# First layer norm of a one-core decoder step: output weights centred before the projection, variance per token, logits from the unscaled sum

## The reference, cut to what matters

```python
merged = g_a * y_a + g_b * y_b + g_c * y_c
m = merged @ w_o
h = layer_norm(ALPHA * x + m, ln1_g, ln1_b)        # mean, variance, rsqrt(var + 1e-5), gain, bias
logits = h @ router_w + router_b                   # (520, 16), softmax, best group of 4, top 2
for e in range(16):
    out += gates[:, e:e+1] * ((silu(h @ w_gate[e]) * (h @ w_up[e])) @ w_down[e])
y = layer_norm(ALPHA * h + out, ln2_g, ln2_b)
```

## Time and profile before

| | us |
|---|---|
| median of 3 runs (lowest, highest) | 1100.54 (1098.97, 1101.18) |
| the profiled execution | 1099.52 |
| its span | 1097.7 |
| TensorE busy | 1001.4 (91%) |
| VectorE busy | 797.5 |
| ScalarE busy | 476.3 |
| GpSimd busy | 349.9 |

### The profile page before, as it was taken

The page is one execution under the profiler, slowest core; times in us unless marked ns, Lnnn a source line. Parts: engine busy times, 40 slices in busy tenths (PEclk is TensorE's granted clock), DMA queues, the critical chain, the costliest instruction groups (busy, mean ns, idle before and its releaser), DMA issues.

```text
span 1097.7 us, 19553 instructions
## 1 busy us (share of the span) xinstructions
PE 1001.4 (91%) x7141; PEld 901.5 (82%) x7141; DVE 797.5 (73%) x960; ACT 476.3 (43%) x661; POOL 349.9 (32%) x268
## 2 busy tenths in 40 slices
PE   6999999999998899999999988974999999999950
PEld 6999999999998789999999988943677777776630
DVE  2398889988898796734335443346789898989969
ACT  3222222222222153335432221263788888787820
POOL 2444444444544242444545443302110000000050
PEclk9999999999999899999999998986999999999985
DMA  7433233323332121422332337655799999999552
GB/s 200 117 97 95 80 93 96 94 82 91 96 96 67 57 87 48 131 88 85 94 98 77 95 89 260 242 213 184 246 358 392 378 381 379 389 391 367 183 195 109
DMA packets 169539, 189.86 MB, mean 173 GB/s; under 512 B 5875, under 2 KB 121587, under 8 KB 169484
## 3 DMA queue, kind: packets, MB, share of 16 engines
q1 hardware_dynamic: 162987, 177.46, 47.9%
q0 software_dynamic: 3008, 10.55, 3.0%
q10 hardware_dynamic: 3505, 1.36, 0.5%
HBM read 178.57 MB, written 11.76 MB: 173 GB/s over the span
## 4 chain that ended last, share of the span: by engine, by line
PE 78%; DVE 10%; issue 4%; DMA 4%; ACT 1%; SPq 1%; POOL 1%; DVEq 0%; POOLq 0%; ACTq 0%
PE pr L891 53%; PE pr L1029 13%; PE work L1029 7%; DVE acc_a L1221 2%; DMA y_rows<-y_out 1%; DMA sb_tok<-in_state_conv_b_dram 1%; PE work L1013 1%; POOL y_a L600 1%; PE work L976 1%; PE work L967 1%; DMA hs<-h_rows,ids 1%; DVE acc_b L1221 1%; PE work L953 1%; DVE stats L1550 1%; DVE y_a L1548 1%
## 5 line engine op out<-in xcount | busy, mean ns | idle before, releaser
L532 POOL TENSOR_TENSOR w_lo<-raw,w_hi 128x512 fp32r<-128x512 f32 x224 | 303.7, 1377 | 394.8 <-ACT w_hi L628 394.8
L891 PE MATMUL pr<-x_hi,w_hi 128*128 128x260 f32 x1280 | 260.1, 284 | 3.1 <-POOL w_lo L532 3.1
L891 PE MATMUL pr<-x_hi,w_lo 128*128 128x260 f32 x1280 | 259.4, 284 | 0.0
L891 PE MATMUL pr<-x_lo,w_hi 128*128 128x260 f32 x1280 | 259.2, 284 | 0.0
L632 ACT ACTIVATE ev<-pr 128x520 f32<-128x520 f32 x104 | 63.0, 605 | 436.3 <-PE pr L891 436.2
L891 PEld LDWEIGHTS pr<-x_hi,w_hi 128*128 128x128 f32 x1280 | 199.4, 190 | 3.5 <-DVE x_lo L1136 3.3
L891 PEld LDWEIGHTS pr<-x_hi,w_lo 128*128 128x128 f32 x1280 | 199.0, 190 | 0.0
L891 PEld LDWEIGHTS pr<-x_lo,w_hi 128*128 128x128 f32 x1280 | 198.4, 190 | 0.0
L1188 DVE SCALAR_TENSOR_TENSOR work<-b_pad,par,work 128x512 f32<-128x512 f32 x224 | 148.2, 746 | 0.0
L628 ACT ACTIVATE w_hi<-raw 128x512 fp32r<-128x512 f32 x224 | 128.2, 624 | 4.8 <-issue 2.4
L563 POOL DMA_INDIRECT hs<-h_rows,ids x16 | 24.2, 1513 | 272.3 <-DVE ids L1413 257.0
(11 more groups left out here) (254 smaller groups left out, 1620.0 us busy)
## 6 DMA issues: line engine op xcount, KB each, us to landing
raw<-in_w_in_dram SPq DMA_DIRECT2D x80, 512.0 KB, 3.7
w_gate<-in_expert_w_gate_dram SPq DMA_DIRECT2D x16, 2048.0 KB, 14.9
w_up<-in_expert_w_up_dram SPq DMA_DIRECT2D x16, 2048.0 KB, 14.0
w_down<-in_expert_w_down_dram SPq DMA_DIRECT2D x16, 2048.0 KB, 13.9
y_rows<-y_out SPq DMA_DIRECT2D x16, 384.0 KB, 12.9
raw<-in_w_a_out_dram SPq DMA_DIRECT2D x8, 512.0 KB, 3.7
raw<-in_w_c_out_dram SPq DMA_DIRECT2D x8, 512.0 KB, 3.7
raw<-in_w_b_out_dram SPq DMA_DIRECT2D x8, 512.0 KB, 3.7
```

Source lines behind the costliest of these rows:

```text
L532: pool.tensor_tensor(w_lo[:, slot, k], raw[:, slot, k], w_hi[:, slot, k].bitcast(F32), ALU.subtract).then_inc(w_split, 1)
L891: mm = pe.matmul(pr[slot][:, h, 0:HALF], w[:, slot, k, :], x[:, k, h * HALF:(h + 1) * HALF], start=(k == 0 and w is w_hi and x is hi), sto ...
```

## The change

The output matrix is loaded whole (`wo`, eight blocks of 512 KB, during the GB pairs) instead of in slices, and VectorE subtracts from each of its rows the row's mean (`centre_weights`). The mean of x over the columns is computed once by 32 matmuls (`meanX`) and subtracted where ALPHA * x is put into `m`. So the projections' sum in `m` has mean zero, and `meanH` and the centring go. VectorE adds the projections straight from PSUM; ScalarE squares each block; VectorE sums the squares. TensorE reduces them per token (token on the partition, 2 columns), root and reciprocal are taken on 5 columns (`r_tok`), and a diagonal matrix per block of tokens spreads the factor to all partitions. The logits are computed from `m` before it is scaled, with router weights times gain; they are scaled by `r_tok` afterwards, and the bias's share (`biasL`) is added. h is written to a buffer of its own (`h_f`). In the router, `posm` takes one operation from the positions in PSUM, and the other copies and the weights of the two experts are computed after the first and second mark. The loads of down for experts 0, 1 and 2 move later, and the rounding of the first gate weights comes after the copies of h. The last GB pairs on ScalarE, the merges on VectorE and the output projections are written out instead of looped.

```diff
 pairs(N_GC, G_C, c_out_v)
-pairs(N_GB, G_B, b_out_v)
+for o in range(KB):
+    load(0, o * 2 + N_GB, in_v, o * P + G_B)
+    load(1, o * 2 + (N_GB + 1), b_out_v, o * P)
+    if o == 1:
+        sp.wait_ge(b_split, KB)
+    if 1 <= o <= 4:
+        for k in (2 * o - 2, 2 * o - 1):
+            sp.dma_start(wo[k // 4][:, k % 4, :], o_v[:, k, :]).then_inc(wo_in[o - 1], 16)
...
+sp.wait_ge(proj_done, 2 + N_WO)
+expert_load(first, 0, TURN[0], "gate")
+expert_load(first, 0, TURN[0], "up")
+sp.wait_ge(z_ready, 1)
+expert_load(first, 1, TURN[1], "gate")
 expert_load(first, 1, TURN[1], "up")
 sp.wait_ge(proj_done, 2 + N_END)
+expert_load(first, 0, TURN[0], "down")
 expert_load(first, 2, TURN[2], "gate")
 expert_load(first, 2, TURN[2], "up")
+h_out()
+sp.wait_ge(first.gathered, 16)
 expert_load(first, 1, TURN[1], "down")
-h_out()
...
+for i in range(KB):
+    for h in range(2):
+        k = slice(h * KB // 2, (h + 1) * KB // 2)
+        pool.wait_ge(w_rounded, (N_WO + i) * 2 + (h + 1))
+        pool.tensor_tensor(w_lo[:, i % 2, k], wo[h][:, :, i * P:(i + 1) * P], w_hi[:, i % 2, k].bitcast(F32), ALU.subtract).then_inc(w_split, 1)
...
-    with act.Fori(0, count // 2) as i:
+def round_wo(i):
+    act.wait_ge(proj_done, N_WO + i + 1)
+    for h in range(2):
+        k = slice(h * KB // 2, (h + 1) * KB // 2)
+        act.wait_ge(wo_centred, KB // 2 * (h + 1))
+        act.activation(w_hi[:, i % 2, k], wo[h][:, :, i * P:(i + 1) * P], ACT.Copy).then_inc(w_rounded, 1)
...
+act.wait_ge(round_done, DONE["meanX"])
+act.activation(halves(x_mean[:]), work[TILE["meanX"]][:, :, 0:HALF], ACT.Copy, scale=ALPHA).then_inc(x_mean_ready, 1)
 root("varB", 1)
...
+act.activation(agg[0:1, 0, 0:1], eps_t[0:1, 0:1], ACT.Sqrt).then_inc(table_ready, 1)
+for i in range(KB):
+    if i < KB - 1:
+        round_wo(i + 1)
+    act.wait_ge(z_ready, i + 1)
+    act.activation(ev[i % 4][:], m[:, i, :], ACT.Square).then_inc(sq_ready, 1)
...
-for k in range(KB):
-    act.wait_ge(h_centred, k + 1)
-    act.activation(sq_h[:, k, :], m[:, k, :], ACT.Square).then_inc(sq_h_ready, 1)
-root("varH", 2)
-rounded_parts(first, "gate", 0, 0, 0, free=range(CH))
-for k in range(KB):
+act.wait_ge(tok_var, 1)
+tok_sq = pr[1][:, 0, 0:2 * NTB].rearrange("p (b c) -> p b c", c=2)
+act.activation(r_tok[:, 0:4].unsqueeze(2), tok_sq[:, 0:4, 0:1], ACT.Sqrt, bias=eps_t[:, 0:1]).then_inc(tok_std, 1)
+act.activation(r_tok[0:TS, 4:5].unsqueeze(2), tok_sq[0:TS, 4:5, 0:1], ACT.Sqrt, bias=eps_t[0:TS, 0:1]).then_inc(tok_std, 1)
+def h_affine(k):
     act.wait_ge(h_white, k + 1)
-    act.activation(m[:, k, :], m[:, k, :], ACT.Identity, scale=par[:, k * NROWS + R_L1G:k * NROWS + R_L1G + 1],
+    act.activation(h_f[:, k, :], h_f[:, k, :], ACT.Identity, scale=par[:, k * NROWS + R_L1G:k * NROWS + R_L1G + 1],
                    bias=par[:, k * NROWS + R_L1B:k * NROWS + R_L1B + 1]).then_inc(h_ready, 1)
+for k in range(4):
+    h_affine(k)
 act.wait_ge(lg_turned, 1)
-act.activation(lg[0:E, :].rearrange("p (h t) -> p h t", h=2), work[TILE["logits"]][0:E, :, 0:HALF], ACT.Copy).then_inc(lg_ready, 1)
+act.activation(lg[0:E, :].rearrange("p (h t) -> p h t", h=2), pr[0][0:E, :, 0:HALF], ACT.Copy).then_inc(lg_ready, 1)
+for k in range(4, KB):
+    h_affine(k)
 act.wait_ge(logits_ready, 1)
...
+rounded_parts(first, "gate", 0, 0, 0, free=range(CH))
...
+pe.wait_ge(mean_rounded, 1)
+work_wait(pe, "meanX")
+for k in range(KB):
+    for x in (x_hi, x_lo):
+        for h in range(2):
+            mm = pe.matmul(work[TILE["meanX"]][:, h, 0:HALF], mean_r[:], x[:, k, h * HALF:(h + 1) * HALF],
+                           start=(k == 0 and x is x_hi), stop=(k == KB - 1 and x is x_lo))
+mm.then_inc(round_done, 1)
 pe.wait_ge(summed, 4)
 mean("varB", sums)
...
+pe.wait_ge(rw_b_ready, 1)
+work_wait(pe, "biasL")
+for k in range(KB):
+    mm = pe.matmul(work[TILE["biasL"]][:, 0, 0:E], mean_w[:], rw_b[:, k, :], start=(k == 0), stop=(k == KB - 1))
+mm.then_inc(round_done, 1)
 pe.wait_ge(merged_split, KB)
-singles(N_WO, q_hi, q_lo)
+for i in range(KB):
+    if i >= 2:
+        pe.wait_ge(z_ready, i - 1)
+    project(i % 2, N_WO + i, q_hi, q_lo, wait_free=i < 2)
...
+pe.wait_ge(rw_ready, 1)
+pe.wait_ge(z_ready, KB - 1)
+def logits(blocks):
+    for k in blocks:
+        for h in range(2):
+            mm = pe.matmul(pr[0][0:E, h, 0:HALF], rw[:, k, :], m[:, k, h * HALF:(h + 1) * HALF],
+                           start=(k == 0), stop=(k == KB - 1))
+    return mm
+logits((0, 1))
 pe.wait_ge(summed, 5)
-mean("meanH", sums)
-work_wait(pe, "varH")
-for k in range(KB):
-    pe.wait_ge(sq_h_ready, k + 1)
-    for h in range(2):
-        mm = pe.matmul(work[TILE["varH"]][:, h, 0:HALF], mean_w[:], sq_h[:, k, h * HALF:(h + 1) * HALF],
-                       start=(k == 0), stop=(k == KB - 1))
-mm.then_inc(round_done, 1)
-pe.wait_ge(late_in, 32)
-work_wait(pe, "logits")
-for k in range(KB):
-    pe.wait_ge(h_ready, k + 1)
-    for h in range(2):
-        mm = pe.matmul(work[TILE["logits"]][0:E, h, 0:HALF], rw[:, k, :], m[:, k, h * HALF:(h + 1) * HALF],
-                       start=(k == 0), stop=(k == KB - 1))
-mm.then_inc(lg_turned, 1)
+for b in range(NTB):
+    n = P if b < 4 else TS
+    mm = pe.matmul(pr[1][0:n, 0, 2 * b:2 * b + 2], sums[:, b * P:b * P + n], mean_w[:, 0:2], start=True, stop=True)
+mm.then_inc(tok_var, 1)
+logits((2, 3))
+pe.wait_ge(diag_ready, 1)
+for b in range(NTB):
+    n = P if b < 4 else TS
+    for lo, hi in ((0, HALF - b * P), (HALF - b * P, n)) if b * P < HALF < b * P + n else ((0, n),):
+        half, at_col = divmod(b * P + lo, HALF)
+        mm = pe.matmul(pr[1][:, half, at_col:at_col + hi - lo], mean_w[0:n, :], diag[0:n, b, lo:hi], start=True, stop=True)
+mm.then_inc(r_spread, 1)
+logits((4, 5, 6, 7)).then_inc(lg_turned, 1)
 pe.wait_ge(lg_ready, 1)
 for b in range(NTB):
     n = P if b < 4 else TS
-    mm = pe.transpose(work[TILE["logits"]][0:n, 0, b * E:(b + 1) * E], lg[0:E, b * P:b * P + n], ident[0:E, 0:E])
-mm.then_inc(round_done, 1)
+    mm = pe.transpose(pr[0][0:n, 0, 272 + b * E:272 + (b + 1) * E], lg[0:E, b * P:b * P + n], ident[0:E, 0:E])
+mm.then_inc(lg_transposed, 1)
+pe.wait_ge(h_ready, KB)
...
-        do(dve.tensor_scalar(blk(m, o), blk(x_hi, o).bitcast(F32), ALPHA, None, ALU.mult))
+        do(dve.scalar_tensor_tensor(blk(m, o), blk(x_hi, o).bitcast(F32), ALPHA, x_mean[:], ALU.mult, ALU.subtract))
...
+def centre_weights(k):
+    part, col_k = wo[k // 4][:, k % 4, :], w_mean[:, k:k + 1]
+    do(dve.tensor_reduce(col_k, part, AX.X, ALU.add))
+    settle()
+    do(dve.tensor_scalar(col_k, col_k, 1.0 / D, None, ALU.mult))
+    settle()
+    dve.tensor_scalar(part, part, col_k, None, ALU.subtract).then_inc(wo_centred, 1)
...
+dve.wait_ge(x_mean_ready, 1)
+for o in range(KB):
+    merge(N_GB, o, o % 2, "last")
+    settle()
+    if 3 <= o < 7:
+        dve.wait_ge(wo_in[o - 3], 32)
+        for k in (2 * o - 6, 2 * o - 5):
+            centre_weights(k)
...
+dve.tensor_tensor(rw[:], rw[:], par_k[:, :, R_L1G:R_L1G + 1].to_broadcast([P, KB, E]), ALU.mult).then_inc(rw_ready, 1)
...
+do(dve.scalar_tensor_tensor(b_logit[:], work[TILE["biasL"]][:, 0, 0:E], float(D), rb[:], ALU.mult, ALU.add), Tally(dve, b_ready))
...
+for i in range(KB):
+    dve.wait_ge(proj_done, N_WO + i + 3)
+    mi = m[:, i, :].rearrange("p (h t) -> p h t", h=2)
+    do(dve.tensor_tensor(mi, mi, pr[i % 2][:, :, 0:HALF], ALU.add), to(z_ready))
+    if i >= 2:
...
-dve.wait_ge(round_done, DONE["meanH"])
+        do(dve.tensor_tensor(sums[:], ev[0][:] if i == 2 else sums[:], ev[(i - 1) % 4][:], ALU.add))
+dve.wait_ge(sq_ready, KB)
+settle()
+do(dve.tensor_tensor(sums[:], sums[:], ev[(KB - 1) % 4][:], ALU.add), to(summed))
+dve.wait_ge(tok_std, 2)
+do(dve.reciprocal(r_tok[:, 0:4], r_tok[:, 0:4]))
+do(dve.reciprocal(r_tok[0:TS, 4:5], r_tok[0:TS, 4:5]))
+settle()
+for b in range(NTB):
+    n = P if b < 4 else TS
+    ins = dve.tensor_scalar(diag[0:n, b, 0:n], ident[0:n, 0:n], r_tok[0:n, b:b + 1], float(D), ALU.mult, ALU.mult)
+    if b < NTB - 1:
+        do(ins)
+    else:
+        ins.then_inc(diag_ready, 1)
+dve.wait_ge(r_spread, 1)
 for k in range(KB):
-    mk = m[:, k, :].rearrange("p (h t) -> p h t", h=2)
-    do(dve.tensor_tensor(mk, mk, work[TILE["meanH"]][:, :, 0:HALF], ALU.subtract), to(h_centred))
-dve.wait_ge(std_ready, 3)
-do(dve.reciprocal(std[:], std[:]))
-settle()
-for k in range(KB):
-    do(dve.tensor_tensor(m[:, k, :], m[:, k, :], std[:], ALU.mult), to(h_white))
+    do(dve.tensor_tensor(h_f[:, k, :].rearrange("p (h t) -> p h t", h=2), m[:, k, :].rearrange("p (h t) -> p h t", h=2),
+                         pr[1][:, :, 0:HALF], ALU.mult), to(h_white))
...
+dve.wait_ge(lg_transposed, 1)
+lg_tok = pr[0][:, 0, 272:272 + NTB * E].rearrange("p (b e) -> p b e", e=E)
+do(dve.tensor_tensor(probs[:, 0:4, :], lg_tok[:, 0:4, :], rep(r_tok[:, 0:4], 2, E), ALU.mult))
+step(dve.tensor_tensor(probs[0:TS, 4, :], lg_tok[0:TS, 4, :], r_tok[0:TS, 4:5].to_broadcast([TS, E]), ALU.mult))
```

(11 more changed lines are left out.)

155 lines of the change are left out of this document (62 added, 93 removed), and 2 rows, old and new, of the table ROUNDS.

## The result

The changed kernel takes **1081.88 us** (median of 4 runs, 1079.82 to 1083.64) against 1099.76 us for the kernel before in the same session (4 runs): ratio 0.9835, 95% interval 0.9814 to 0.9857. The forecast was 1087.5 (1083.0 to 1094.0): faster, as said, but by 17.9 us instead of 13, and 1.1 us outside the range. The profiled execution took 1081.94 us, its span is 1079.9 (1097.7 before).

A forecast was written before the change was run, and what follows sets the result against it. TensorE was busy 91%, but 54.5 us before the first expert product passed in one-at-a-time hand-overs. 3.2 + 1.3 - 17.5 = -13.0 from 1099.52 gave 1086.5; with 1.0 for the median, 1087.5 us (1083 to 1094).

The forecast's parts named there:

- Term 1: Mean of x: 32 matmuls near 407 us and the ScalarE series behind them delay the spatial matmuls, +3.2 us.
- Term 2: Centring w_o on VectorE in the last merges delays the copy and meets GpSimd once more: +1.3 us (0.4 to 3).
- Term 3: From the last output projection to the first expert product, the rebuilt norm and router save time: -17.5 us.
- rival 1: The clock drops in the new norm, slowing variance, spread and last logits: about 5 us reaches exp, 1092.5; chance 0.16.
- rival 2: Stores of h set the first gather, behind slow transposes and queued stores: 2.5 us, 1090; chance 0.14.
- rival 3: Loads of w_o blocks starve the weight slices, stalling TensorE in four groups: 23 us in all, 1110; chance 0.04.

The follow-up runs named there:

- e7: The changed kernel without the mean of x (matmul group, copy and subtraction left out; computes another result): 1077.67 us, ratio to the kernel before 0.9821.
- e14: The kernel before, with GpSimd's low parts of the second output-weight block waiting for VectorE's last merge and split: 1094.68 us, ratio 0.9976.
- e13: The changed kernel, with GpSimd making most low parts of the output weights only after VectorE's last merge and split: 1077.43 us, ratio to before 0.9825.
- e2: The kernel before, with the nine weight-picking operations moved between the marks and the gate subtractions: 1094.72 us, ratio 0.9979.
- e1: The changed kernel with the nine weight-picking VectorE operations moved behind the four gate subtractions: 1085.31 us, ratio to the kernel before 0.9897.
- e12: e8 with twelve unread products put into TensorE's wait ahead of the transposes of h: 1075.68 us, ratio to the kernel before 0.9802.
- e8: The changed kernel with the mean of x computed in TensorE's pause ahead of the output projections: 1075.87 us, ratio to the kernel before 0.9805.
- e15: e8 plus GpSimd's low parts of the output weights waiting for VectorE's last merge and split: 1075.35 us, ratio to the kernel before 0.9803.
- e5: The changed kernel again, unaltered, as base for a later session: 1082.17 us, ratio to the kernel before 0.9848.
- e9: The changed kernel plus an unread copy of the 32 mean-of-x products in the pause ahead of the output projections: 1078.94 us, ratio to before 0.9829.

## Why the prediction was right or wrong

**The direction and the place were right**, and so were most of the steps: the new norm and router take the time out between the last output projection and the first expert product, at full clock; the centring hides in the gated stage; the experts take as long as before.

**Term 1 (+3.2)** measured +2.98 between the two profiles, and +3.36 with the scatter of the stage before it left out (e7). The sum over ScalarE's series was the right way to get it.

**Term 2 (+1.3, from 0.4 to 3)** measured +0.46, near the lower bound. My working had the last copy half a microsecond late and one more meeting with GpSimd. The copy wasn't late: centring ended at 658.31, the product at 658.77. The one more meeting came: two stretched operations became three, and the loss grew from 1.70 us (5.63 against e14's 3.93) to 2.67, so by 1.0 for my 0.8. What I hadn't counted is that without any meeting the pause got 0.5 shorter (3.93 in e14, 3.41 in e13): the last merge and the output projections are no longer run in loops, the gaps of 0.11 to 0.14 us between the four operations shrank to 0.03, and TensorE begins 0.04 us behind the last one instead of 0.33. So the 0.46 is 1.0 - 0.5 and not the 0.5 + 0.8 of my sum; that it meets my lower bound, which stood for "no new meeting", is luck. What I didn't see is that the meeting in the kernel before was itself a loss that could be had back. I read the 1.57 against 0.70 as a price to be added, and not as a cost that already stood in the pause. With the clock that it pulls down behind it, it is worth 4.5 to 5.2 us in the changed kernel (e13), more than terms 1 and 2 together. The rule of the Trainium skill, page "SBUF — State Buffer", section "Who interferes with whom", as I read it (every centring subtraction caught by GpSimd) would have given 3; the trace shows 0.46. Two of the eight subtractions were stretched (1.82 and 1.89 against 0.75), both in the gated stage, where TensorE was not idle from 430 to 655 us.

**Term 3 (-17.5)** measured -20.88, and this is the step that put the forecast outside its range. The sentence that failed is the one that lets the weights be picked "beside the 8.25 us gather". I took that duration as a property of the gather. It was the time of an undisturbed one and 3.7 us of waiting for VectorE's gate subtractions; and I had even placed these subtractions on VectorE at that moment, asking when VectorE would be free and not whom they met. The change puts nine small operations in front of them, and the gather goes first. A second step failed with it: I put the later loads of down at "nothing". With the short record they are worth 1.3 us, since with the old place of these loads the gather took 5.84 us (e2) and in the change 4.57 (4.19 to 4.93 in the other profiles with its order); without this the change's gather would have lost part of what the order gave. e1 restores the old meeting and nothing else, and gives a tail of 37.33 us, against my 37. So the rest of term 3's working holds to a third of a microsecond in its sum. Single items were off by 0.3 to 0.4 and cancelled: the ten short matmuls took 1.18 (0.9 forecast), the spread 1.71 (1.3).

**The sum.** 2.98 + 0.46 - 0.15 - 20.88 - 0.2 = -17.8. Against my -13.0, term 3 makes 3.4 of the difference, term 2 makes 0.8, and term 1, projections and experts 0.2 each. The forecast of 1087.5 stood another 1.0 above the profiled execution's sum, for the first median; in the session of the result that was 0.2. With term 3 alone set right the forecast would have been about 1084, inside its range.

**The rivals.** The clock (rival 1) stayed at 1.00 through the norm and the logits and first fell at 728 us, where transposes follow a wait of 2.4 us. There e12 shows it off the path but for 0.7 at most. The stores (rival 2) do set the gather, at 738.29 against ids that were ready at 737.83, as near as I had said. The weight slices (rival 3) weren't starved: TensorE never idles from 430 to 655 us. The root at 412.41 starts 0.01 us after its table load ends, as before, and exp starts at 729.11, 0.01 us after its load (727.82, 1.28 us). The drain of 1.38 us that the Trainium skill, page "ScalarE: Activation LUTs", section "What ACT_TABLE_LOAD costs", adds doesn't show here either.

**Versions that beat both kernels.** e8, e12 and e15 compute the same result in 1075.4 to 1075.9 us, 6.3 to 6.8 below the change; they can't be told from one another. e8 is the simplest of them. e13 (1077.4) does it with one added wait.

## What to carry to other kernels

A duration read from a trace is that of the instruction in its company. Before carrying one into a new schedule, look at what ran beside it and whether it still will, above all for GpSimd next to VectorE, and for a gather next to loads on the same DMA engines. Where an engine waits for a short chain, compare each link with the same form elsewhere in the trace: a stretched link is a gain that no added or removed instruction shows. And a necessary pass of TensorE was cheapest where it would have idled otherwise: in e8 that gave back its 3.36 us and some 2 us of slow clock behind the pause.

## What the runs showed of the hardware

- GpSimd's record of an indirect gather took 1.09 us undisturbed. It took 4.71 to 5.32 us when four back-to-back VectorE subtractions (both inputs in SBUF) had begun 0.44 to 1.06 us ahead of it, and ended about one whole undisturbed record after the last of them. VectorE lost nothing (4.62). Begun 0.23 us behind the gather, they cost it nothing, though both ran side by side for 0.86 us (e5).
- Copies (one input) of the same tiles did the same for as long as they ran (2.65 us).
- VectorE's operations of 520 columns and GpSimd's subtractions stretch in meeting: 0.70 to 1.37 and 1.64, 0.43 to 1.49 us.
- The granted clock was at its 0.50 level for 5.4 us of the output projections behind 4.4 us of waiting (the change), for some 3.3 us behind 3.9 us (e14), and stayed at 1.00 behind 1.7 us (e13). In e9 it was at 0.50 for 3.4 us although TensorE waited for only 0.57 us; the last 1.85 us before were 16-column products. In e9 and e14 it fell 0.6 to 0.7 us after the projections had begun, with TensorE busy. What it goes by isn't settled here.
- The gather's 384 KB landed 3.0 to 3.8 us behind its record where the load queue was empty, and 4.75 us behind it in e2, where a 2 MB load filled the DMA engines (share 1.02).
